# ScalarE in place of GpSimd for the high parts of the down-projection weights

## The reference

```python
h = rmsnorm(x, p['norm_mlp'][layer])
x = x + (jnp.square(jax.nn.relu(h @ p['mlp_up'][layer])) @ p['mlp_down'][layer]).astype(dt)
```

## Time and profile before

| what | value |
|---|---|
| median of three runs | 3393.47 us (3390.40 to 3399.25) |
| the profiled execution | 3389.58 us, its span 3387.8 us |
| granted TensorE clock, mean | 0.984 of full speed |
| busy PE, DVE, ACT, POOL | 3245.1, 1955.3, 1002.8, 1046.3 us |
| down phases in the span | about 1616 to 1986 us and 3001 to 3374 us |

### The profile page before, as it was taken

The page is one execution under the profiler, slowest core; times in us unless marked ns, Lnnn a source line. Parts: engine busy times, 40 slices in busy tenths (PEclk is TensorE's granted clock), DMA queues, the critical chain, the costliest instruction groups (busy, mean ns, idle before and its releaser), DMA issues.

```text
span 3387.8 us, 71544 instructions
## 1 busy us (share of the span) xinstructions
PE 3245.1 (96%) x30948; PEld 3079.2 (91%) x30948; DVE 1955.3 (58%) x3060; ACT 1002.8 (30%) x1989; POOL 1046.3 (31%) x544
## 2 busy tenths in 40 slices
PE   7999889999999999999999989999999999999998
PEld 6999768888887889999999989999988899999998
DVE  5112875665665667444666674565556844456667
ACT  3344133333333335444100142122222444420002
POOL 3322120110113035445334423222211544444431
PEclk9999899999999999999999999999999999999999
DMA  5113630010011112333323201211221133333221
GB/s 169 57 58 107 191 121 13 24 36 15 24 36 53 60 48 89 102 102 115 125 97 101 76 32 51 71 58 58 71 99 65 57 105 112 112 136 101 88 90 71
DMA packets 100491, 270.55 MB, mean 80 GB/s; under 512 B 11272, under 2 KB 44724, under 8 KB 100056
## 3 DMA queue, kind: packets, MB, share of 16 engines
q1 hardware_dynamic: 55792, 190.60, 16.6%
q10 hardware_dynamic: 44392, 75.42, 6.5%
HBM read 201.17 MB, written 67.17 MB: 79 GB/s over the span
## 4 chain that ended last, share of the span: by engine, by line
PE 77%; DVE 7%; issue 2%; ACT 1%; DMA 1%; POOL 0%; ACTq 0%; DVEq 0%
PE psum L798 21%; PE psum L247 19%; PE psum L766 18%; PE psum L2411 2%; PE psum L3425 2%; PE psum L2428 1%; PE psum L2199 1%; PE psum L2385 1%; PE psum L2465 1%; PE psum L2327 1%; PE psum L2398 1%; PE psum L2431 1%; DMA act_lo<-c_lo 1%; DVE c_ks L3667 1%; DVE s_sc L1865 0%
## 5 line engine op out<-in xcount | busy, mean ns | idle before, releaser
L247 PE MATMUL psum<-act_hi,w_hi 128*128 128x352 f32 x2088 | 703.5, 337 | 25.8 <-DVE act_lo L342 12.1
L247 PE MATMUL psum<-act_hi,w_lo 128*128 128x352 f32 x2088 | 676.8, 324 | 0.0
L247 PE MATMUL psum<-act_lo,w_hi 128*128 128x352 f32 x2088 | 675.6, 324 | 0.0
L232 POOL TENSOR_TENSOR w_hi<-w_raw,derived 128x1024 fp32r<-128x1024 f32 x87 | 173.7, 1997 | 1421.9 <-PE psum L247 1307.0
L1141 DVE TENSOR_TENSOR x<-x,psum 128x352 f32<-128x352 f32 x768 | 391.0, 519 | 250.4 <-PE psum L798 250.4
L798 PE MATMUL psum<-ff_u_hi,w_hi 128*128 128x352 f32 x1536 | 498.6, 325 | 4.4 <-DVE ff_u_lo L1104 4.4
L798 PE MATMUL psum<-ff_u_lo,w_hi 128*128 128x352 f32 x1536 | 496.7, 323 | 0.0
L798 PE MATMUL psum<-ff_u_hi,w_lo 128*128 128x352 f32 x1536 | 496.4, 323 | 0.0
L247 PEld LDWEIGHTS psum<-act_hi,w_hi 128*128 128x128 f32 x2088 | 396.6, 190 | 54.8 <-issue 14.9
L247 PEld LDWEIGHTS psum<-act_lo,w_hi 128*128 128x128 f32 x2088 | 397.9, 191 | 2.2
L247 PEld LDWEIGHTS psum<-act_hi,w_lo 128*128 128x128 f32 x2088 | 397.0, 190 | 0.0
(11 more groups left out here) (508 smaller groups left out, 5639.7 us busy)
## 6 DMA issues: line engine op xcount, KB each, us to landing
ff_raw<-mlp SPq DMA_DIRECT2D x128, 512.0 KB, 4.2
w_raw<-weights SPq DMA_DIRECT2D x87, 512.0 KB, 3.7
u<-ff_stage SPq DMA_DIRECT2D x64, 528.0 KB, 2.9
ff_u_raw<-u SPq DMA_DIRECT2D x64, 528.0 KB, 4.6
s_cache<-cache_a ACTq DMA_DIRECT2D x32, 512.0 KB, 7.1
kv<-a_qkv ACTq DMA_DIRECT2D x12, 528.0 KB, 2.7
x<-x_in ACTq DMA_DIRECT2D x8, 528.0 KB, 4.8
y<-end_y SPq DMA_DIRECT2D x12, 352.0 KB, 2.4
```

Source lines behind the costliest of these rows:

```text
L232: pool.tensor_tensor(hi, raw, self.zeros, ALU.add).then_inc(s.sem, s.step())
L247: last = pe.matmul(out, w[:, k, :], h[:, k, cols], start=(start and k == ks[0] and m == 0), stop=(stop and k == ks[-1] and m == 2))
```

## The change

ACT copies the raw weight tile into `hi` in place of GpSimd's addition of zeros, with the waits that GpSimd had; GpSimd waits for that copy and does the subtraction alone. ACT's order becomes `square_out` 12, the two copies of group 0, `u_high(0, 0)`, `u_high(0, 1)`, `square_out` 21; and for later groups a copy stands ahead of each `u_high(g, q)`.

```diff
+    def down_high(self, act, g, q):
+        K, n, at = self.K, self.n, self.K.plan.at
+        s = K.plan.steps["act"]
+        hi = K.slots[self.down_slot(g, q)][0].rearrange("p k c -> p (k c)")
+        end = self.PAIRS - 1
+        if g >= 2:
+            act.wait_ge(*at(self.group_end(g - 2)))
+        elif g == 1:
+            act.wait_ge(*at(f"pe.{n}.{end}.P{3 if q == 0 else 7}.1"))
+        elif q == 0:
+            act.wait_ge(*at(f"pe.{n}.{end}.P2.1"))
+        else:
+            act.wait_ge(*at(f"dve.{n}.{end}.S4"))
+        act.wait_ge(K.sem(f"{n}_raw{q}"), 16 * (self.PAIRS + g + 1))
+        act.activation(hi, self.raw[q][:, :], ACT.Copy).then_inc(s.sem, s.step(f"act.{n}.d{g}.whi{q}"))
...
     def down_split(self, pool, g, q):
...
-        pool.wait_ge(K.sem(f"{n}_raw{q}"), 16 * (self.PAIRS + g + 1))
-        pool.tensor_tensor(hi, raw, K.zeros, ALU.add).then_inc(s.sem, s.step(f"split.{n}.d{g}.hi{q}"))
-        pool.wait_ge(*at(f"split.{n}.d{g}.hi{q}"))
-        pool.tensor_tensor(lo, raw, hi.bitcast(F32), ALU.subtract).then_inc(s.sem, s.step(f"split.{n}.d{g}.lo{q}"))
+        pool.wait_ge(*at(f"act.{n}.d{g}.whi{q}"))
+        pool.tensor_tensor(lo, self.raw[q][:, :], hi.bitcast(F32), ALU.subtract).then_inc(s.sem, s.step(f"split.{n}.d{g}.lo{q}"))
...
         self.square_out(act, w, "12")
         for q in range(2):
+            self.down_high(act, 0, q)
+        for q in range(2):
             self.u_high(act, 0, q)
         self.square_out(act, w, "21")
         for g in range(1, self.GROUPS):
             for q in range(2):
+                self.down_high(act, g, q)
                 self.u_high(act, g, q)
```

## The result

The changed kernel takes 3410.33 us in the median of 9 runs (3402.1 to 3417.06), the kernel before 3397.11 us in 9 runs (3390.4 to 3400.82). The ratio is 1.0037 with a 95% interval of 1.0023 to 1.0050: 0.0037 x 3397 = 12.6 us slower, with 8 to 17 possible. A second series of the same kernel gave 1.0034 (1.0018 to 1.0050). The forecast was 9.5 us. The profiled execution took 3413.07 us with a span of 3411.0 us, 23 us over that of before; how little of the 23 belongs to the change is told with the last experiment.

The account below looks back on a forecast made before the run. PE was taken to bound the down phase. Handovers 9.0, clock 0 and group 0 0.5 summed to 9.5 us on the median 3393.47, giving 3403.0 us, 0.28% slower; range 3394 to 3410 us.

Parts of the forecast that it names:

- Removed: worth nothing.: Down phase: taking 64 additions, 121.6 us, off GpSimd gains nothing on the path, being hidden by PE's matmuls.
- Added: 1.05 us a copy, no cost in the later groups.: 14 later groups of each MLP: ScalarE's 1.05 us copies cost nothing, with 4 us of cover on ACT.
- At the handover, 4.5 us each.: Up to down phase: GpSimd and DVE low parts alternate under an exclusive lock, PE starts 4.5 us later, 9.0 for both.
- The overlap rival: Handover: DVE and GpSimd run side by side, only GpSimd's queue costs, 2.3 us each, 3398 us; chance 0.14.
- The clock: 0.: Behind the longer handover wait: PE's slow clock loses nothing more, 0 us, within half a microsecond each.
- Group 0, 0.5 us near tile 14.: First MLP: copy (1, 0) waits for its raw tile, addition 8 comes late, PE waits 0.5 us; second MLP nothing.
- GpSimd goes twice, the third rival: Group 0: GpSimd's two group 1 subtractions run back to back, delaying DVE; 14.9 us in all, 3408 us; chance 0.19.

Follow-up runs that it names:

- the last experiment: The changed kernel and the kernel before, both unedited, each run once more with its own profile; ratios 1.0034 and 1.0000 against the kernel before.
- groups only: Kernel before, with ScalarE copying high parts for groups 1 to 15 only and GpSimd still splitting group 0; ratio 1.0007, then 0.9997.
- copies early: Changed kernel with group 0's two weight copies moved up behind `square_out` 11 in ScalarE's order; ratio 1.0001 against the kernel before.
- handover only: Changed kernel with ScalarE copies for group 0 of each MLP alone, groups 1 to 15 as before; ratio 1.0041 against the kernel before.
- the reordered kernel: Kernel before, no ScalarE copies, group 0's `u_high` ahead of `square_out` 22, `u_low` behind quadrants 22 and 12; ratio 0.9971, then 0.9979.
- with `u_high` first: Changed kernel with both `u_high` of group 0 ahead of its two weight copies on ScalarE; ratio 1.0038 against the kernel before.

## Why the prediction was right

Point by point, by its own steps:

- *Removed: worth nothing.* Right within what groups only can tell: 1.0007 and 0.9997. The rows for it were the earlier trace rows.
- *Added: 1.05 us a copy, no cost in the later groups.* Right: 1054 ns, ScalarE done 4.0 us behind a group's start, no wait.
- *At the handover, 4.5 us each.* Right: 6.59 - 2.21 = 4.4 us at both, by the forecast mechanism, with the second low part of u at 3.4 us. GpSimd's queue alone gave 2.3, ScalarE's alone 1.9. The overlap rival is out: it wanted a wait of about 4.5 us and no instruction that stands behind another engine's. The Trainium skill, "SBUF — State Buffer", section "SBUF: two separate sides", has the exclusive lock that is held for a whole instruction; the trace agrees, by the 3.39 us of a low part that takes 1.25 alone, and by 6.8 us on two engines against 4.7 on one.
- *The clock: 0.* This term was mis-sized. I took from a single row, the 0.66 behind the 6.3 us wait at L247, that a longer wait loses only what is lost already. From the start of the down phase's first matmul to that of its thirty-first it is 4.8 us where PE did not wait. Behind the 2.2 us waits (before and groups only, two profiles each, and copies early) it is 6.4 to 6.5 us in eight cases of ten, and 4.9 in the other two (one handover each in the second profiles of before and of groups only). Behind the six waits of 6.6 us (changed, twice, and handover only) it is 7.4, 7.4, 6.2, 6.9, 6.3 and 7.4 us. By the means, 6.1 and 6.9, that is 0.8 us more for each handover, beyond the half microsecond that the prediction gave as the end; in the changed kernel's first profile it is 1.0.
- *Group 0, 0.5 us near tile 14.* It did not come in the changed kernel, because the raw tile was there sooner than the prediction had carried over. Copy (1, 0) started 8.4, 8.1, 9.3 and 9.2 us behind PE's first matmul in the four groups 0 of the two profiles, and not 10.7. Addition 8 was done at 13.5, 13.2, 14.4 and 14.3, and tile 14 began only at 16.1, 16.1, 14.8 and 15.5, without a wait. Where the tile was late, the wait came: 0.3 us in the second profile of groups only, with the copy at 10.4. It also came, 1.1 and 0.6 us, in the kernel whose PE starts without a slow stretch and so reaches tile 14 sooner. The mechanism was right; when the tile lands was the term that missed, and one profile could not give it: the kernel before's own first split of group 1 started 10.7 us behind PE in its first profile and 8.6 in its second. The copy (1, 0) of the changed kernel's first profile, that of the second profile of groups only, and PE's wait there:

```profile
1642.68 1.06 ACT L725 ACTIVATE w_hi<-ff_raw 128x1024 fp32r<-128x1024 f32 x1 [6.64 <-DMA ff_raw<-mlp]
```

```profile
1631.98 1.06 ACT L725 ACTIVATE w_hi<-ff_raw 128x1024 fp32r<-128x1024 f32 x1 [8.63 <-DMA ff_raw<-mlp]
```

```profile
PE psum L818 <- DVE x L1162: 0.3, 1, 0.3
```

- *GpSimd goes twice, the third rival:* out. In group 0 of both profiles of the changed kernel DVE's low part (1, 0) ran between GpSimd's two subtractions.

Sum: 2 x 4.4 + 2 x 0.8 of clock = 10.4 us. The MLP stages agree: 1445.3 us in the mean of the three profiles with waits of 6.6 us, 1434.9 in the mean of the five with waits of 2.2, 10.5 us apart. The timed ratios of the two series say 12.6 and 11.5, with intervals of 8 to 17 and 6 to 17. The forecast of 9.5 us lies inside them, in part by luck: it had 0.5 us for a wait in group 0 that did not come and nothing for the clock, which cost 1.6. It put the border of 0.3% just above itself, and the measured median lies just beyond. In absolute terms the changed kernel's 3410.33 us is 0.3 us above the written range of 3394 to 3410. The forecast had built on a median of 3393.47 us in three runs of before, which came out at 3397.11 in nine; the measured ratio on the first of the two is 3406 us. Of the 23 us between the two spans, 13.8 lie ahead of the first MLP and are no part of this.

## What to carry to other kernels

Before an engine is relieved, ask who waits for it: 123 us taken off GpSimd bought nothing. And 4 of 64 moved instructions cost it all: they came so late in an in-order queue that GpSimd's subtractions, which hang on them, fell on the same microseconds as VectorE's low parts, with PE waiting for both. To turn the order round at that place did not help. When work moves to another queue, it should go where that queue idles; the same copies about ten microseconds earlier were free. And a wait that the trace of before already shows at such a place is worth an experiment of its own: here a reordering that had nothing to do with the change took away the 2.2 us waits, the slow clock behind them, and 0.2 to 0.3% of the time.

## What the runs showed of the hardware

- The fall of TensorE's clock behind a wait is no fixed price; what decides it no run here shows. Behind a wait of 2.2 us the windows of before show 0.56 and 0.59. In the second profile of the same kernel, behind the same wait at the second handover, there is no fall at all (first matmul at 3009.72):

```profile
3009.00:3011.00 2.00, 1.28 (x8) 1.31 (x9) 1.83 (x4) 0.14 (x1) 0.00 (x0) 1.00 0.00 0
3011.00:3013.00 2.00, 2.00 (x15) 2.00 (x14) 1.13 (x3) 0.51 (x1) 0.00 (x0) 1.00 0.36 139
```

- Two executions of one program differ by 10 us (before) and 16 us (the reordered kernel, 1276.2 and 1292.6) at the start of the first MLP. A difference of two spans says little at 0.3%; stretches between two points of one stage agree within 2 to 3 us.
- At the handover GpSimd and VectorE took turns instruction by instruction, even though GpSimd's second subtraction was ready (since 1628.08) before its first had ended (1629.57). Summed as if on one engine, the four instructions gave 4.5 us, and 4.4 was measured. The sum must hold every VectorE instruction that gets in: with `u_high` first it was one more, and the end came 0.5 us later.
- Not every VectorE instruction is held off. L1098, which reads PSUM and one tile of SBUF, took its usual 0.70 us at 1624.69 while GpSimd's subtraction ran beside it; L1103, from two tiles of SBUF, took 2.11 in place of 0.71 right behind it.
